# Placing every SBUF tile at a multiple of 64 bytes, with rows of 1088 instead of 1032 bytes for the normalised activations

## What is computed

```
h = h + hybrid_mixer(rmsnorm(h)); h = h + memory_attention(h, mem); h = h + swiglu(rmsnorm(h)); x = rmsnorm(h)
x = x + gate_m * mix(rms(x)*(1+scale_m)+shift_m)        # forgetting attention and retention
x = x + gate_f * (relu(h @ w_mlp_in)**2 @ w_mlp_out)    # h = rms(x)*(1+scale_f)+shift_f
```

## The kernel before, in words

| tile | start | size | start modulo 64 |
|---|---|---|---|
| raw | 16384 | 32768 | 0 |
| hi, lo | 49152, 73728 | 24576 each | 0 |
| h (with the small columns) | 98304 | 8672 | 0 |
| u_hi, u_lo | 106976, 115232 | 8256 each | 32 |
| work, rstd_bc, ones, ..., mem_scale (18 tiles) | from 123488 | | 32 |
| the stage tiles: merged, mixed, hid_hi; proj; mem_t_hi; turned_hi | 162240; 162240; 187456; 203840 | | 0 |

## Time and profile before

### The profile page before, as it was taken

One profiled execution on the slowest core, in us unless ns is written; L12 is line 12 of the kernel. 1 busy time (PEld: TensorE's weight loads), 2 busy tenths in 40 slices (PEclk: granted clock), 3 DMA queues, 4 the chain that ended last, 5 costly groups with the idle time before them and its releaser, 6 DMA issues.

```text
span 801.1 us, 15067 instructions
## 1 busy us (share of the span) xinstructions
PE 769.5 (96%) x6410; PEld 755.1 (94%) x6410; DVE 594.1 (74%) x869; ACT 378.1 (47%) x509; POOL 23.6 (3%) x22
## 2 busy tenths in 40 slices
PE   8999998999899999999999999999989999999998
PEld 8999987899788999999999999989989899999998
DVE  5555778877886778998898788975966878755563
ACT  6657345553655634333344546426554543433431
POOL 0000000002001000000000000200000000000000
PEclk9999998999999999999999999999999999999999
DMA  9733363331734448989987336555334277855511
GB/s 339 296 146 116 121 236 106 106 110 64 301 109 155 157 160 345 363 309 309 328 297 271 106 136 225 210 192 176 107 103 170 99 274 265 300 175 193 198 66 54
DMA packets 24115, 156.10 MB, mean 195 GB/s; under 512 B 3568, under 2 KB 3696, under 8 KB 6000
## 3 DMA queue, kind: packets, MB, share of 16 engines
q1 hardware_dynamic: 24048, 155.13, 54.0%
HBM read 154.07 MB, written 1.05 MB: 194 GB/s over the span
## 4 chain that ended last, share of the span: by engine, by line
PE 63%; DVE 17%; issue 10%; ACT 8%; DMA 1%; POOL 0%; SPq 0%; DVEq 0%; POOLq 0%; ACTq 0%
PE bank L737 12%; PE bank L739 12%; PE bank L738 12%; PE bank L810 6%; PE bank L813 6%; PE bank L812 6%; ACT sb_hi L1330 4%; DVE sb_lo L1661 4%; PE bank L745 2%; PE bank L748 2%; PE bank L747 2%; DVE sb_masked L2030 1%; DMA sb_raw<-in_stream 1%; PE bank L1196 1%; DVE sb_gates L1672 1%
## 5 line engine op out<-in xcount | busy, mean ns | idle before, releaser
L1661 DVE TENSOR_TENSOR sb_lo<-sb_raw,sb_hi 128x2048 fp32r<-128x2048 f32 (+1 forms) x116 | 262.0, 2261 | 126.9 <-ACT sb_hi L1330 126.3
L1330 ACT CAST sb_hi<-sb_raw 128x2048 fp32r<-128x2048 f32 (+1 forms) x116 | 217.7, 1882 | 113.8 <-PE bank L813 56.1
L737 PE MATMUL bank<-sb_u_hi,sb_hi 128*128 128x256 f32 (+2 forms) x800 | 228.6, 286 | 0.0
L739 PE MATMUL bank<-sb_u_hi,sb_lo 128*128 128x256 f32 (+2 forms) x800 | 225.9, 282 | 0.0
L738 PE MATMUL bank<-sb_u_lo,sb_hi 128*128 128x256 f32 (+2 forms) x800 | 225.2, 282 | 0.0
L737 PEld LDWEIGHTS bank<-sb_u_hi,sb_hi 128*128 128x128 f32 (+2 forms) x800 | 150.5, 188 | 3.3 <-issue 2.5
L738 PEld LDWEIGHTS bank<-sb_u_lo,sb_hi 128*128 128x128 f32 (+2 forms) x800 | 150.7, 188 | 0.4
L739 PEld LDWEIGHTS bank<-sb_u_hi,sb_lo 128*128 128x128 f32 (+2 forms) x800 | 150.4, 188 | 0.2
L810 PE MATMUL bank<-sb_hid_hi,sb_hi 128*128 128x256 f32 x432 | 119.7, 277 | 0.4 <-DVE sb_hid_lo L1715 0.4
L812 PE MATMUL bank<-sb_hid_lo,sb_hi 128*128 128x256 f32 x432 | 119.4, 276 | 0.0
L813 PE MATMUL bank<-sb_hid_hi,sb_lo 128*128 128x256 f32 x432 | 119.4, 276 | 0.0
(11 more groups left out here) (352 smaller groups left out, 1180.8 us busy)
## 6 DMA issues: line engine op xcount, KB each, us to landing
sb_raw<-in_stream SPq DMA_DIRECT2D x140, 1024.0 KB, 5.1
sb_raw<-in_stream SPq DMA_DIRECT2D x4, 256.0 KB, 6.6
sb_raw<-in_stream SPq DMA_DIRECT2D x2, 512.0 KB, 8.6
sb_mem_t<-in_mem SPq DMA_DIRECT2D x1, 1024.0 KB, 4.8
out<-sb_h SPq DMA_DIRECT2D x4, 256.0 KB, 2.2
sb_const<-in_constants SPq DMA_DIRECT2D x1, 830.0 KB, 11.0
sb_h<-in_x SPq DMA_DIRECT2D x1, 572.0 KB, 3.8
sb_h<-in_x SPq DMA_DIRECT2D x1, 512.0 KB, 6.6
```

The source lines that it names most:

```text
L737: nc.tensor.matmul(out, a_hi, b_hi, start=(i == 0), stop=False)
L739: last = nc.tensor.matmul(out, a_lo, b_hi, start=False, stop=(i == n - 1))
L1330: nc.scalar.copy(hi[:, s % SPLIT, 0:n], x[:, 0:n]).then_inc(sem("hi_ready"), 1)
L1661: tt(lo[:, s % SPLIT, 0:n], x[:, 0:n], f32(hi[:, s % SPLIT, 0:n]), ALU.subtract) \
```

## The change

Every tile is asked for at a multiple of 64 bytes; `u_hi_x` and `u_lo_x` get rows of 272 floats (1088 bytes, 17 times 64), and the one place that reads past column 256 takes 258 columns of them as before; the scratch for dynamic DMAs shrinks from 16384 to 4096 bytes. No instruction is added, removed or resized.

```diff
-            return stack.enter_context(nc.sbuf_tensor("sb_" + name, shape, dt))
+            return stack.enter_context(nc.sbuf_tensor("sb_" + name, shape, dt, align_bytes=64))
...
-        u_hi_x = sb(ctx, "u_hi", [P, KD, T + 2], F32R)
-        u_lo_x = sb(ctx, "u_lo", [P, KD, T + 2], F32R)
+        u_hi_x = sb(ctx, "u_hi", [P, KD, T + 16], F32R)
+        u_lo_x = sb(ctx, "u_lo", [P, KD, T + 16], F32R)
...
-                                                           [(u_hi_x[:, k, :], u_lo_x[:, k, :])]))
+                                                           [(u_hi_x[:, k, 0:T + 2], u_lo_x[:, k, 0:T + 2])]))
...
-    nc = bacc.Bacc("TRN2", target_bir_lowering=False, num_devices=1)
+    nc = bacc.Bacc("TRN2", target_bir_lowering=False, num_devices=1,
+                   dynamic_dma_scratch_size=4096)
```

## The result

The changed kernel takes 809.88 us (median of 6 runs, 809.37 to 811.21) against 804.12 us for the kernel before (6 runs, 803.14 to 806.15). The ratio is 1.0075, with an interval of 1.0063 to 1.0086: slower by 0.75%, where 786 us and a gain of 2% were forecast. The profiled execution of the changed kernel took 809.83 us, 6.97 more than that of before.

What follows compares the result with a forecast made beforehand. PE was taken as the bound, strictly in the feed-forwards. Gains of 9.2 (feed-forwards), 7.9 (other stages) and 0.7 us (aligned matmuls) sum to 17.8, from 802.86 to 785.1, plus 1.25 to the median: 786 us, range 783 to 805.

Steps and rivals of the forecast that it cites:

- The bound: Whole kernel: PE limits; in the two feed-forwards, 358 us, every nanosecond between matmuls is paid in full, elsewhere most.
- rival D: All products: loop order (`accumulate` against `by_feature`), not addresses, sets the distance; no effect, 804 us; chance 0.09.
- At the fast level of 113.4 ns a moving one saves 118.75 - 113.4 = 5.3 ns, a stationary one 118.3 - 113.4 = 4.9.: Products with `u`: 2,544 moving and 1,152 stationary matmuls reach the pace of fast aligned operands.
- the 9.2 + 7.9 = 17.1 of the sum: `u` products: 9.2 us gained in the feed-forwards, 7.9 in other stages, taken as 80% of 9.9.
- rival C: `u` products: only irregularity goes, `u` reaches the slow level, `hid` stays; 3.0 us gained, 801 us; chance 0.15.
- moves all tiles down by the same amount: Smaller DMA scratch: only makes room and shifts every tile equally; no time term.
- Cost nothing: Smaller DMA scratch: nothing uses it, since SP issues all transfers; no time lost.
- if the new base of the stage tiles moves `hid` off its level: Stage tiles: closing condition under which the prediction would be wrong; given no size.
- Rival E: Feed-forwards: regular `u` lets the slow level run on and take `hid` along; 808 us, at worst 812; chance 0.12.
- The term for `merged`, `mixed` and `mem_t`: Some 320 aligned slow matmuls, `turned` included: half of a possible 1.4 us gained, 0.7.
- DVE and ACT: Instructions touching odd-start tiles: about 3 ns each, left out of the sum; bounds 0 and 1 us gained.

Runs made afterwards that it cites:

- The matmul rows by themselves: Separate kernel with only float32r matmul rows, operand distance varied, no other engine working; 113.2 ns between starts at 448, 118.7 at 384, 119.8 at 512, 120.0 at 0.
- all at 192: Changed kernel with 1280-byte `u` rows, `u` and `hid` both 192 modulo 256 from the weights: median 799.20 us over nine executions, ratio 0.9926 to the kernel before.
- 1152-byte rows: Changed kernel with `u` rows of 1152 bytes and 64 bytes before `u_hi`: 796.55 us, ratio 0.9913 to the kernel before; run again 798.39 us, 0.9922.
- The kernel with the weights moved: Changed kernel with weights up 64 bytes and everything behind them up 128: 802.28 us, ratio 0.9982 to the kernel before.

## Why the prediction was wrong

**The bound** was read rightly: PE's distance between starts is paid in full in the feed-forwards, and 5 ns on 1,296 `hid` matmuls came through as 6 to 7 us. That the pace depends on the operands' places and not on the order of the loop (against rival D) was right too.

**The failed step: "At the fast level of 113.4 ns a moving one saves 118.75 - 113.4 = 5.3 ns, a stationary one 118.3 - 113.4 = 4.9."** Moving `u` saved 0.8 ns and stationary `u` nothing: 2.0 us instead of the 9.2 + 7.9 = 17.1 of the sum. The step took a multiple of 64 for the property that parts `hid` from `u`. It is the distance from the other operand: `hid` had 192 modulo 256. `u` at a multiple of 64 begins at 0 modulo 128, one of the slow places, and its 1088-byte rows step on by 64, so that only every other row lies at 64 modulo 128. The matmul rows by themselves give 117.5 for it. The row that could have told was cited under rival C and given too little weight: k = 4 of `u` starts at a multiple of 64 and was as slow as any. From the weights it lies 111104 - 49152 = 61952 bytes, 0 modulo 256, the slowest of the four places. And that place is not enough either: at 64 modulo 256 with rows of 1280 bytes moving `u` stayed at 117.8 in the feed-forwards, and only all at 192 gave it 113.3 there, in the one execution traced. Case C, forecast at 3.0 us gained, is what `u` did, with 2.0.

**The second failed step: the scratch "moves all tiles down by the same amount", and the sum has no term for `hid`.** "Cost nothing" was right for the scratch (0.9999). But the change as a whole does not move all tiles by the same amount. The longer rows (2 x 8 x 56 = 896 bytes) and the rounding (64) moved the stage tiles 960 bytes farther from the weights, from 192 to 128 modulo 256. That cost 6.7 us, undone by 64 bytes. The prediction named it in its last sentence, "if the new base of the stage tiles moves `hid` off its level", and under rival E only as something that acts through the level of the neighbour. It gave it no term. The rows had the price: with `hid` at the pace of today's `u`, 1,296 x 5 = 6.5 us, the greater part of the worst case of rival E.

**Rival E** gave 808 to 812 and the time lies there, but its mechanism is wrong. It had regular `u` leaving PE on the slow level; with the stage tiles moved and `u` unchanged, `hid` is fast again. The matmuls ahead do act on the level of a row, but only where both levels exist, at 64 modulo 128. That the time fell between 808 and 812 is luck.

**The term for `merged`, `mixed` and `mem_t`**, 0.7 us gained, was 1.5 lost, for the same reason as `hid`.

**DVE and ACT** were rightly left out: 594.1 and 594.4 us busy, 378.1 and 378.3.

**The rules of the Trainium skill.** With no other engine at work, matmuls of one shape ran 113.2, 117.9, 118.7 and 120.0 ns apart at four distances. The Trainium skill, SBUF — State Buffer, section "Who interferes with whom", has PE never waiting on anyone and two independent read ports; this case's runs disagree with independence of the two operands, since moving either one changes the speed. The Trainium skill, SBUF — State Buffer, section on Door 1, gives SBUF lines of 16 bytes; by these alone the distances 384, 448 and 512 would be equal, and they measured 118.7, 113.2 and 119.8.

**Left open**: what in PE or SBUF makes the places differ; by what rule a row at 64 modulo 128 enters the fast or the slow level, since the same row behind the same 24 matmuls was seen on both; and, with it, why stationary `u` averages 114.4 with 1152-byte rows and 117.6 in the profiled execution with all at 192.

## What to carry to other kernels

Where PE is the bound, measure the distance between matmul starts for each kind of operand pair, and compare it with where the two tiles lie to each other, modulo 128 and 256: in this kernel that was worth 4 to 6% of a matmul, and any edit that resizes a tile changes it for all tiles behind it. A change of alignment is therefore priced over every operand it moves, not only over those it means to improve. A kernel that sits on one of two levels should be timed over many executions: with all operands at 192 the best one (792 us) and the median (799 us) differ by more than the change under test.

## What the hardware showed unexpectedly

- Float32r matmuls of 128 x 128 by 256 columns start 113.3 or 117.8 ns apart when moving and stationary operand lie 64 modulo 128 bytes apart, 118.6 to 118.8 at 128 modulo 256, and 119.6 to 120.0 at 0 modulo 256, with no other engine at work.
- At 64 modulo 128 both levels are stable. The same row ran at 117.7 or 113.7 behind other rows, and once at 113.4 behind the kind of row that had left it at 117.7; two rows of 192 held 113.4.
- The mean granted clock differs between executions of one kernel, and the time with it. The kernel with the weights moved took 800.9 to 801.6 us at a clock of 0.996, 803.9 to 804.0 at 0.991 and 806.1 to 806.3 at 0.987: 5 us between the ends, nearly as much as the whole effect of this change. So small ratios here rest on the medians of several runs, and the placement on the distances in the trace.
